# Loading the mixture-of-experts weights earlier and in another order behind a fused mixer on one Trainium2 core

## What is computed

```
z = rms_norm(x) @ w_in                      # 1024 x 4096, split in u, q, k, v, two gates
y_ssm = glu(gelu(S5(u)))                    # chunked state-space scan, then w_glu (512 x 512)
y_att = diff_attention(q, k, v)             # 4 heads, chunk-causal
mixed = sig(g_ssm) * (y_ssm @ w_proj_ssm) + sig(g_att) * (y_att @ w_proj_att)
h = x + mixed @ w_out
hn = rms_norm(h)
# router: top 4 of 32 experts for each token
for each expert e:                          # rows of the tokens that chose e
    act = swiglu(rows @ w_up[e] + b_up[e])  # w_up[e]: 1024 x 2048, 8 MB
    out += weight * (act @ w_down[e] + b_down[e])   # w_down[e]: 1024 x 1024, 4 MB
y = h + out
```

## Time and profile before

| | us |
|---|---|
| median of 3 runs (1145.76 to 1146.14) | 1146.06 |
| span of the profiled execution | 1142.5 |
| PE busy in it | 1095.7 (96%) |
| DVE, ACT, POOL busy | 298.4, 166.3, 34.1 |
| data moved by DMA | 435.13 MB, mean 381 GB/s |
| TensorE clock granted | full in all 40 slices |

### The profile page before, as it was taken

One profiled execution on the slowest core, in us unless ns is written; L12 is line 12 of the kernel. 1 busy time (PEld: TensorE's weight loads), 2 busy tenths in 40 slices (PEclk: granted clock), 3 DMA queues, 4 the chain that ended last, 5 costly groups with the idle time before them and its releaser, 6 DMA issues.

```text
span 1142.5 us, 14277 instructions
## 1 busy us (share of the span) xinstructions
PE 1095.7 (96%) x5292; PEld 446.9 (39%) x5292; DVE 298.4 (26%) x804; ACT 166.3 (15%) x343; POOL 34.1 (3%) x51
## 2 busy tenths in 40 slices
PE   7999999999999999999999999999999999999997
PEld 4468887633333333333333333333333333333332
DVE  5987244242111111111111111111111111111111
ACT  3043440221111111111111111111111111111110
POOL 6020010000000000000000000000000000000000
PEclk9999999999999999999999999999999999999999
DMA  8734489999999999999999999999999999999996
GB/s 229 200 123 87 140 284 352 366 361 403 427 428 427 429 430 427 429 430 428 428 430 429 427 430 427 428 430 427 428 430 428 427 430 429 427 430 429 427 428 269
DMA packets 63578, 435.13 MB, mean 381 GB/s; under 512 B 19856, under 2 KB 28096, under 8 KB 38592
## 3 DMA queue, kind: packets, MB, share of 16 engines
q1 hardware_dynamic: 57776, 433.17, 92.6%
q0 software_dynamic: 608, 1.34, 0.6%
q10 hardware_dynamic: 5168, 0.27, 0.3%
HBM read 432.01 MB, written 1.57 MB: 380 GB/s over the span
## 4 chain that ended last, share of the span: by engine, by line
PE 58%; DMA 38%; DVE 2%; ACT 1%; issue 1%; SPq 0%; DVEq 0%; ACTq 0%
DMA arena<-in_w_up 38%; PE bank L1066 23%; PE bank L1111 9%; PE bank L635 5%; PE bank L673 4%; PE bank L619 3%; PE bank L1010 2%; PE bank L995 2%; PE bank L949 2%; PE bank L873 1%; PE bank L858 1%; PE bank L846 1%; DMA arena<-in_w_in 1%; PE bank L805 1%; PE bank L937 1%
## 5 line engine op out<-in xcount | busy, mean ns | idle before, releaser
L1066 PE MATMUL bank<-arena 128*64 128x512 f32 x2048 | 452.6, 594 | 30.2 <-DMA arena<-in_w_up 29.9
L1066 PEld LDWEIGHTS bank<-arena 128*64 128x64 f32 x2048 | 143.7, 137 | 331.8 <-issue 271.5
L1111 PE MATMUL bank<-arena 128*64 128x512 f32 x1024 | 226.8, 595 | 0.0
L1809 DVE TENSOR_SCALAR arena<-bank 128x256 f32<-128x256 f32 x64 | 27.2, 425 | 499.1 <-PE bank L1066 499.1
L1111 PEld LDWEIGHTS bank<-arena 128*64 128x64 f32 x1024 | 70.7, 137 | 133.9 <-issue 133.1
L1367 ACT ACTIVATE arena<-arena 128x256 f32<-128x256 f32 x64 | 26.6, 417 | 451.7 <-DVE arena L1810 451.7
L619 PEld LDWEIGHTS bank<-arena 128*128 128x128 f32 (+1 forms) x450 | 49.2, 143 | 89.6 <-issue 82.1
L619 PE MATMUL bank<-arena 128*128 128x128 f32 (+1 forms) x450 | 75.2, 290 | 8.9 <-DMA arena<-in_x 5.1
L1010 PE MATMUL bank<-arena 64*128 64x512 f32 x256 | 63.9, 616 | 0.7 <-ACT arena L1375 0.7
L995 PE MATMUL bank<-arena 128*64 128x512 f32 x248 | 60.1, 605 | 0.0
L1774 DVE TENSOR_SCALAR arena<-arena 128x128 f32 (+3 forms) x126 | 33.3, 327 | 92.7 <-issue 92.6
(11 more groups left out here) (294 smaller groups left out, 517.0 us busy)
## 6 DMA issues: line engine op xcount, KB each, us to landing
arena<-in_w_up SPq DMA_DIRECT2D x125, 2048.0 KB, 25.5
arena<-in_w_down SPq DMA_DIRECT2D x63, 2048.0 KB, 26.8
arena<-in_w_in SPq DMA_DIRECT2D x16, 1024.0 KB, 6.0
arena<-in_w_up SPq DMA_DIRECT2D x5, 1024.0 KB, 6.4
arena<-in_w_out SPq DMA_DIRECT2D x4, 1024.0 KB, 7.8
arena<-in_w_proj_ssm SPq DMA_DIRECT2D x8, 256.0 KB, 5.8
arena<-in_w_proj_att SPq DMA_DIRECT2D x2, 1024.0 KB, 7.9
arena<-in_w_down SPq DMA_DIRECT2D x2, 1024.0 KB, 31.6
```

The costliest lines, as they stand in the source:

```text
L1066: last = pe.matmul(B[n][64 * h:64 * h + 64, :], xg[:, 2 * j + r, :], rows[r][2 * h + n], start=False, stop=(j == order[-1] and r == 1), sk ...
L1111: last = pe.matmul(B[3][64 * n:64 * n + 64, :], (actT_last if last_block else actT)[:, k % 4, k // 4, :], dn_w[parity][k // 4][:, k % 4, 5 ...
L1809: TS(part(glu_t, n), v[:, 0], LIMIT, None, ALU.min)
```

## The change

SP's loop now ends with piece 15. What follows is written out: wait for `y_ps` 2 alone, then expert 0's up tiles 0 and 1 ahead of piece 16, up tile 2 behind it, up tile 3 behind piece 17; behind piece 18, after `yT_ps` 2, expert 0's down tile 1; then piece 24; after `wt` 8 expert 1's down tile 0; then piece 19, expert 0's down tile 0, pieces 20 and 21, and the rest. Expert 1's up tile 2 is loaded as two rows: row 0 after `mixed` 4, row 1 after `out_ps` 5; PE waits for row 0 with a semaphore of its own (`row_in`). The bias loads `bup` move ahead of `out_ps` 3. The mixer's temporary `mtmp` moves from 176 KB to 108 KB, which frees the home at 176 KB for expert 1's down tile 0.

```diff
-        mtmp = at(176, 2, 2 * TOK)
+        mtmp = at(108, 2, 2 * TOK)
...
-            ups_after = {17: (0,), 18: (1,), 19: (2,), 23: (3,)}
-            downs_after = {23: (1, 0)}
-
-            for i in (*range(21), PIECES - 1, *range(21, PIECES - 1)):
+            for i in range(16):
...
-                if i == 16:
-
-                    sp.wait_ge(s["y_ps"], 1)
-                    sp.wait_ge(s["yT_ps"], 2)
-                for k in ups_after.get(i, ()):
-                    load_up_tile(0, 0, 0, k)
-                if i == 21:
-                    sp.wait_ge(s["oT"], 1)
-                    load_up_tile(1, 1, 1, SHARED + 1)
-                for j in downs_after.get(i, ()):
-                    load_dn(0, 0, 0, j)
...
+            def load_piece(i):
+
+                sp.wait_ge(piece_used, 16 if i == PIECES - 1 else i - RING + 1)
+                for dst, src in piece(i):
+                    sp.dma_start(dst, src).then_inc(last_in if i == PIECES - 1 else slot_in[i % RING], 16)
...
+            sp.wait_ge(s["y_ps"], 2)
+            load_up_tile(0, 0, 0, 0)
+            load_up_tile(0, 0, 0, 1)
+            load_piece(16)
+            load_up_tile(0, 0, 0, 2)
+            load_piece(17)
+            load_up_tile(0, 0, 0, 3)
+            load_piece(18)
+            sp.wait_ge(s["yT_ps"], 2)
+            load_dn(0, 0, 0, 1)
+            load_piece(PIECES - 1)
+            sp.wait_ge(s["wt"], 8)
+            load_dn(1, 1, 1, 0)
+            load_piece(19)
+            load_dn(0, 0, 0, 0)
+            load_piece(20)
+            load_piece(21)
+            sp.wait_ge(s["oT"], 1)
+            load_up_tile(1, 1, 1, SHARED + 1)
+            load_piece(22)
+            load_piece(23)
             sp.wait_ge(s["mixed"], 4)
+            load_row(up_w[1][SHARED][:, 0], 1, 0, SHARED).then_inc(s["row_in"], 16)
             load_ahead_part(3)
-            load_dn(1, 1, 1, 0)
-            sp.wait_ge(s["out_ps"], 3)
             for q in range(4):
                 sp.dma_start(bup[E * q:E * q + E], b_up[:, 512 * q:512 * q + 512]).then_inc(bup_in, 16)
+            sp.wait_ge(s["out_ps"], 3)
             load_dn(1, 1, 1, 1)
             sp.wait_ge(s["out_ps"], 5)
-            load_up_tile(1, 1, 1, SHARED)
+            load_row(up_w[1][SHARED][:, 1], 1, 1, SHARED).then_inc(up_in[1][SHARED], 16)
             load_ahead_part(2)
...
+                        if ahead and j == SHARED:
+                            pe.wait_ge(s["row_in"], 16)
                         pe.wait_ge(up_in[parity][j], 8 * b + (8 if parity else 16))
```

More of the change, by code:

```diff
@@ L61 @@
  sig act aT2_ps aT2 ysb summed up_used dn_used bup_used dsel fin fin_out wr_in loop_z u_turn
- ahead_in up_tail dn_tail wg gated first_rows row_left row_right cT g1_in gate_ps out_ps rank routed o_read row_used up_half warm""".split()
+ ahead_in up_tail dn_tail wg gated first_rows row_left row_right cT g1_in gate_ps out_ps rank routed o_read row_used up_half warm row_in""".split()
 def mixer_and_experts(nc, a, out):
@@ L353, in _ @@
                                 .then_inc(s["m_in"], 16)
-                if i == PIECES - 1:
-                    sp.wait_ge(piece_used, 16)
-                elif i >= RING:
+                if i >= RING:
                     sp.wait_ge(piece_used, i - RING + 1)
-                arrived = last_in if i == PIECES - 1 else slot_in[i % RING]
+                arrived = slot_in[i % RING]
                 if i > 0:
@@ L391, in _, with load_row @@
                               .then_inc(s["vec_in"], 16)
-                if i == 16:
-                    sp.wait_ge(s["y_ps"], 1)
-                    sp.wait_ge(s["yT_ps"], 2)
-                for k in ups_after.get(i, ()):
-                    load_up_tile(0, 0, 0, k)
-                if i == 21:
-                    sp.wait_ge(s["oT"], 1)
-                    load_up_tile(1, 1, 1, SHARED + 1)
-                for j in downs_after.get(i, ()):
-                    load_dn(0, 0, 0, j)
-            def load_row(dst, e, r):
-                return sp.dma_start(dst, w_up[e, 0:2 * P, :].rearrange("(p r) (h n) -> r p h n", r=2, h=2)[r])
+            def load_piece(i):
+                sp.wait_ge(piece_used, 16 if i == PIECES - 1 else i - RING + 1)
+                for dst, src in piece(i):
+                    sp.dma_start(dst, src).then_inc(last_in if i == PIECES - 1 else slot_in[i % RING], 16)
+            def load_row(dst, e, r, j=0):
+                return sp.dma_start(dst, w_up[e, 2 * P * j:2 * P * (j + 1), :]
+                                    .rearrange("(p r) (h n) -> r p h n", r=2, h=2)[r])
             def load_ahead_part(q):
```

## The result

| | before | after |
|---|---|---|
| median of the runs, us | 1146.06 (1145.29 to 1146.83, 5 runs) | 1164.48 (1164.20 to 1165.49, 5 runs) |
| ratio to before | | 1.0159 (95%: 1.0147 to 1.0171) |
| span of the profiled execution, us | 1142.5 | 1162.7 |
| start of block 0 on PE, us | 232.30 | 252.22 |
| span less start of block 0, us | 910.2 | 910.5 |

What follows compares the result with a forecast made beforehand. DMA was taken as the bound from about 460 us, its full-rate stretch started by a home PE gives back. Stalls of 6.1 + 0.5 = 6.6 us made 1146.06 into 1152.7, range 1147.0 to 1156.5.

Steps and rivals of the forecast that it cites:

- The anchor: Expert blocks: the end is PE's giving back of up tile 1's home plus fixed bytes; earlier mixer loads gain 0.
- The small parts at nothing: `mtmp` in another room, one more PE wait, `bup` sooner: 0 each, with 0.1 us either way.
- The waits for pieces 19 and 20: PE's line 858: a stall of 6.1 us for piece 19 and 0.5 more for piece 20 at tile 4.
- The waits for pieces 16 and 18: Ahead of line 858: no stall; piece 16 just met at 149.55, piece 18 met by 4 us.
- The replay of the queue: SP's queue served in order from 132.3, landings summed from units per load: piece 19 at 185.2, piece 20 at 192.7.
- The first tile on an idle queue: Start of SP's queue: up tile 0 takes 7.8 us at most, landing at 140.1.
- The tile unit of 4.9 and the 128-partition piece of 2.6: SP's queue: a 2 MB tile behind others takes 4.9 us, a 1 MB piece over 128 partitions 2.6 us.
- The router's small loads: POOL's loads issued when `yg` is ready, ahead of piece 19: 1.9 us lost, bounds 0 and 3.3.
- The 32-partition piece of 4.5 us: SP's queue: a 1 MB piece of four 32-partition DMAs, pieces 16 to 18, takes 4.5 us.
- The bounds: Loss between 4.7 us with the router's loads free and 8.8 with all dear: 1150.7 to 1154.9.
- The "no stall" rival: Quarter pieces let the next tile through, costing 2.45 us and not 4.5; stall about 0.6, 1146.7; chance 0.12.
- Span and median: From predicted span 1149.1 to the median: 3.6 us that lie between them added, giving 1152.7.

Runs made afterwards that it cites:

- early_no_stall: Changed kernel with tiles still begun at `y_ps` 2, but each piece put ahead of the tile that would make it late: 1147.42 us, ratio 1.0018.
- old_order_2: Changed kernel with its loads truly in the order of before, piece 16 ahead of the two waits, rest of the change kept: 1145.47 us, ratio 0.9988.
- four_full: Changed kernel with pieces 16 to 18 still loaded by four DMAs each, but each DMA over all 128 partitions: 1148.46 us, ratio 1.0018.
- old_order: Changed kernel with the new load order undone, except that piece 16 stood behind the two waits: 1150.75 us, ratio 1.0035.
- whole_pieces: Changed kernel with pieces 16 to 18 each loaded by one DMA over 128 partitions in place of four over 32: 1149.00 us, ratio 1.0023.
- pe_delay: Kernel before with 15 more 128x256 products on PE just ahead of block 0, 6.5 us in all: 1152.84 us, ratio 1.0055.
- pieces_first: Changed kernel with its first seven loads kept, then piece 19 first and expert 1's two tiles last: 1153.63 us, ratio 1.0061.
- busy_waits: Changed kernel with useless products on PE where it waits, 5 ahead of line 859's second half and 20 ahead of line 871: 1162.11 us, ratio 1.0143.
- halves64: Changed kernel with pieces 16 to 18 each loaded by two DMAs over 64 partitions: 1163.22 us, ratio 1.0145.
- turned_quarters: Changed kernel with the four DMAs of each of pieces 16 to 18 issued in partition order 0, 64, 32, 96: 1164.22 us, ratio 1.0151.

## Why the prediction was right in kind and wrong in size

**The anchor: right, and shown.** The end was to be the time at which PE gives a home back, plus a fixed number of bytes. Span less start of block 0 in the profiles:

| kernel | block 0 starts | span | difference |
|---|---|---|---|
| before | 232.30 | 1142.5 | 910.2 |
| early_no_stall | 234.18 | 1144.2 | 910.0 |
| old_order_2 | 234.63 | 1145.0 | 910.4 |
| four_full | 234.74 | 1145.1 | 910.4 |
| old_order | 236.69 | 1147.2 | 910.5 |
| whole_pieces | 237.09 | 1147.3 | 910.2 |
| pe_delay | 240.66 | 1151.3 | 910.6 |
| pieces_first | 243.01 | 1153.2 | 910.2 |
| busy_waits | 245.96 | 1156.3 | 910.3 |
| halves64 | 251.60 | 1162.0 | 910.4 |
| turned_quarters | 252.15 | 1162.5 | 910.3 |
| after | 252.22 | 1162.7 | 910.5 |

The start of block 0 varies by 20 us, the difference by 0.6. And `early_no_stall` shows that bytes moved ahead of block 0 gain nothing.

**The small parts at nothing: right.** `old_order_2` holds them all and is at 0.9988, some 1.4 us faster than before, with an interval whose upper end is 0.2 us below it.

**The waits for pieces 19 and 20: right in place, if not in form.** The wait for piece 19 is there, 6.49 us. That for piece 20 is not: PE came to tile 4 at half clock, 1.1 us after the landing. But the landing of piece 20 still sets the end of line 871, so that what PE loses ahead of it does not count.

**The waits for pieces 16 and 18: not forecast.** Piece 16 was to be in at 149.5 and piece 18 at 168.3, four us before it is needed. Less the 2.25 us of the profiled execution they landed at 152.4 and 178.4. PE's 2.58 and 2.76 us come from the late first tile and from the same mis-sized term as the rest, below. They lie ahead of the wait for piece 19, which would have been longer without them.

**The replay of the queue: the step that failed.** It had piece 20 at 192.7. Shifted by the 2.25 us of the profiled execution that is 194.95; measured is 204.8, 9.9 us later. By its terms:
- *The first tile on an idle queue*, 7.8 us: measured 9.0, 1.2 more. The row used was that of a lone load at 270.6. A long idle time is not the reason: the changed kernel's load at 234.5, alone on a queue that had been idle for 10 us, lands in 7.8 us again. Up tile 0 has another tile queued right behind it and lands in 8.9 us in `whole_pieces` and `four_full` too. That the load behind it is the cause is not shown.
- *The tile unit of 4.9 and the 128-partition piece of 2.6*: right where nothing disturbs them. With `whole_pieces` the replay by its own units gives 3 x (4.5 - 2.6) = 5.7 less than 52.6, or 46.9; measured 47.5. There up tile 1 lands 5.0 us after up tile 0, piece 16 in 2.7 more, up tile 2 in 4.9.
- *The router's small loads*, 1.9: it is in that sum, which comes out. In `whole_pieces` expert 1's down tile 0, on which they fall, takes 179.26 - 172.75 = 6.5 us in place of 4.9, so 1.6 (POOL issues them from 168.4 us on, and DMA moves 233 GB/s from 176 to 178).
- *The 32-partition piece of 4.5 us*: this is the term that was mis-sized. 61.3 - 47.5 = 13.8 us for three pieces, or **4.6 us each above the 2.6 of a plain piece, where the replay had 1.9**. A piece of this form costs the queue 7.2 us, not 4.5. The unit was read from the earlier trace rows as the landing of the piece behind that of the tile ahead of it. So read it still holds (154.7 - 150.2 is 4.5). What it misses is that the tile itself is late when such a piece is queued right behind it: up tile 1 lands 150.2 - 143.5 = 6.7 us after up tile 0 in place of 4.9, up tile 2 lands 162.24 - 154.68 = 7.6 us after piece 16, and up tile 3 175.7 - 166.8 = 8.9 after piece 17. The unit began its count at that late landing.

**The bounds were wrong for the same reason.** The range took both ends of the router's loads and none of the piece's, which was taken as measured. It was measured with one tile ahead of it in the queue, not with two or three. In `early_no_stall`, where piece 18 again comes when little more than one tile is ahead, it takes 166.28 - 161.65 = 4.6 us and the tile 161.65 - 156.53 = 5.1. The "no stall" rival asked whether the quarters let the tiles through; what happened is the opposite.

**The clock: missing.** After its waits of 2.58, 2.76 and 6.49 us PE worked at half clock for a time. No term stood for it. On the path it is 1.0 us, by the working above.

Together: 6.6 + 9.9 + 1.0 = 17.5 of the 17.67 us measured from the chunk outputs to block 0.

**Span and median.** The 3.6 us added between them was not a constant: the changed kernel has 1164.48 - 1162.7 = 1.8. The 1.8 holds for before too (a run of 1144.07 us has a span of 1142.3), so its profile was of an execution faster than its median. It didn't matter, since the same was taken off and put on.

**What stays open** is why each quarter piece costs 2.7 us more than the 1.9 for the ports that a 32-partition write leaves out. The 4.6 is that of one profile: with the same pieces `turned_quarters` has 60.2 us from up tile 0 to piece 20 and `busy_waits` 58.6, which makes 4.2 and 3.7 a piece.

The traces do show that the queue falls out of step. Each load raises its semaphore 16 times, once for each part of it. In the changed kernel three quarters of the updates of piece 18 were in by 173.3 us, before the last of up tile 3 ahead of it in the queue at 175.7, and the remaining quarter was complete only at 180.6. Of piece 20 fourteen updates came from 199.3 to 201.1 and the last two at 203.3 and 204.8; in `whole_pieces` fourteen came from 187.4 to 188.1 and the last two at 189.4 and 189.6.

So parts of a quarter piece overtake the tile ahead of it, while others lag, which the replay, with one load behind the other, could not have. This lag of the last part makes some 2 of the 13.8 us; the rest falls on all parts. DMA engines that are at different loads of the queue and write to the same ports would do it, but that is argued. The runs show that the form of the piece is the cause, and that neither the number of its DMAs nor the order of its quarters matters; they do not show how.

## What to carry to other kernels

Before moving loads ahead in a queue, ask what starts the stretch in which DMA is the bound: if it is a buffer that an engine gives back, loads ahead of it gain nothing, and what they delay on that engine's path costs its full price. In one queue in order, the latest time of each small urgent load has to be checked against the sum of all that is put ahead of it. A unit for that sum should be read where the queue is as deep as it will be, and loads that write less than all 128 partitions are to be charged for what they do to their neighbours, and best not put among large ones at all.

## What was not expected of the hardware

- A 1 MB load written in ranges of 32 partitions, queued among 2 MB tiles, cost the queue 7.2 us in the changed kernel (6.3 and 6.8 in two other profiles with such pieces) and 7.0 in ranges of 64. The same load over 128 partitions took 2.6 to 2.7, whether in one DMA or in four. DMA moved 262 and 280 GB/s in place of 394 in that stretch, with the same share of busy engines (1.04 to 1.05).
- After a wait of 2.58 us the granted clock of PE fell to 1.2 GHz for a few us; after waits of 2.62 and 2.72 us at the same place in other runs it did not. Of 5.8 us of longer work only 1.0 lay on the path, as the rest was paid out of the next wait.
